# Attention values weighed per key head, high and low part side by side

## The chip, the cores and the metric

The kernel runs on one core of one Trainium2 chip. Its engines work side by side, each through its own list of instructions in order: TensorE (PE in the profile, its weight loads PEld), VectorE (DVE), ScalarE (ACT) and GpSimd (POOL); SyncE (SP) issues DMAs. They meet at semaphores. The metric is the device time of one execution in microseconds. Before the change it is 1051.31 us, the median of 3 runs (1051.22 to 1051.55).

## The reference

One decoder layer on 512 tokens of width 1024 in float32: a gated feed-forward half step, then pooling and attention side by side, merged by gates, then a second feed-forward half step. The change lies in attention, of which this is the core:

```python
q = rmsnorm(q, q_norm); k = rmsnorm(k, k_norm)          # 16 query heads, 2 key heads, width 64
# blocks of 128 queries; each sees its own 128 keys and the 128 before
scores = jnp.einsum('bnqhgd,bnkhd->bnhgqk', qb, kk) * (HEAD_DIM ** -0.5)
scores = jnp.where(mask, scores, finfo.min)
probs = softmax(concatenate([scores, sink], -1))[..., :-1]
out = jnp.einsum('bnhgqk,bnkhd->bnqhgd', probs, vv)     # the step that is changed
```

The result goes through w_attn_out, is gated, added to the pooling branch and multiplied by w_out.

## The kernel before

**Numbers in two parts.** The matmuls take operands in the format that the code calls F32R, not plain float32. Each matrix is split into a high part (the copy in that format, made by ScalarE) and a low part (what is left, made by VectorE or GpSimd), and a product takes three passes: high by high, high by low, low by high.

**Steps of attention.** The 512 tokens are four blocks of 128 queries (nb = 0 to 3). In each, four steps (j = 0 to 3) take four heads each: two query heads of either key head (kv). Block 0 has only its own 128 keys, the others 256. A step on TensorE (`step`, L909) is: the scores of step s (L877), half of a gate projection (24 products of 512 columns in all, L538 to L540), the turning of the probabilities of step s-1 (L891), the other half of the gate, and the weighing of the values by the probabilities of step s-1 (`weigh`, L894 to L907). The gate projections have nothing to do with attention's heads; they are work put between.

**The other engines in a step.** VectorE: maxima of the masked scores of step s (`maxima`, L1957 to L1973), low part of the turned probabilities of s-1 (L1998), denominators (L1978, L1980), scaling of the gate (L1985), and last the low part of the weighed values of s-1 (`attn_part`, L2005). In the step with j = 0 a copy of the block's factors (`rq_now`, L1950) comes ahead of the maxima. ScalarE: high part of the turned probabilities of s-1 (L1361), four exponentials of s (L1345), the high part of the next weights (L973), tanh of the gate (L1355), and last the high part of the weighed values of s-1 (L1367). GpSimd: the division of the probabilities (L1495), then the low part of the next weights (L1429), an instruction of about 2.4 us. Which engine does what, and in which order, is written out by hand in the code; the first and last blocks are written out, the middle ones run in a loop of the hardware.

**Weighing.** Before the change `weigh` multiplies both key heads at once. Of each half of the keys the stationary block holds the values of both key heads (128 columns), and the moving operand 512 columns of probabilities (2 key heads by 2 query heads by 128 queries). Only the rows of a key head that meet its own columns are used, so half of each product is thrown away. It waits for the low part of the turned probabilities (`pt_low`) and for the bank of the last step to be read out (`attn_low`).

**After attention.** TensorE begins the output projection (unit U_AO, L935 to L944) between the last steps: tiles 0 to 3 need the steps j = 0 and 1 of the last block, tiles 4 and 5 its step 2, tiles 6 and 7 its step 3. The wait ahead of the first tiles is L936.

Of the kernel before, what the change touches and what calls it, by code (L numbers as in the profile page):

```python
# [25 lines left out]
F32R = mybir.dt.float32r  # L26
ALU = mybir.AluOpType
ACT = mybir.ActivationFunctionType

P = 128  # L30
# [8 lines left out]
HD = 64  # L39
KV = 2  # L40
QT = 8
BLK = 128
NB = TOK // BLK
# [53 lines left out]
M_GATE_W = M_RINV + TOK * 4  # L97
# [24 lines left out]
def layer_kernel(nc, x_in, consts_in, params_in, poolw_in, weights_in, out):  # L122
    ctx = ExitStack()
    with ctx:
        def put(name, shape, at, dt=F32):

            return nc.alloc_sbuf_tensor_at(name, shape, dt, offset=at)

        def sem(name):
            return ctx.enter_context(nc.semaphore(name))  # L130
# [56 lines left out]
        m = M_GATE_W  # L187
        gate_w = blocks("gate", m, (m + 4096, m + 8192), m + 12288, m + 14336, (m + 16384, m + 18432),
                        m + 20480, m + 24576, m + 28672, m + 30720, m + 32768)
        m = M_RAW  # L190
# [10 lines left out]
        m = M_MIX  # L201
# [8 lines left out]
        m = m + 32768  # L210
# [4 lines left out]
        m = m + 6144  # L215
# [5 lines left out]
        m = m + 32768  # L221
# [10 lines left out]
        ks_l = put("k_block_low", [P, 2 * BLK], m + 21504, F32R)  # L232
        vs_h = put("v_block_high", [P, 2, P], m + 22528, F32R)
        vs_l = put("v_block_low", [P, 2, P], m + 23552, F32R)
        smax, msink, smx, nmax, rows, esink, den, rden = [
# [86 lines left out]
        pt_low = sem("pt_low_done")  # L322
        weighed = sem("weighed")
        attn_high = sem("attn_high_done")
        attn_low = sem("attn_low_done")
# [49 lines left out]
        def is_first(nb):  # L375
            return isinstance(nb, int) and nb == 0
# [5 lines left out]
        def halves(nb):  # L382

            return (1,) if is_first(nb) else (0, 1)

        def turned_count(nb, j):

            return j if is_first(nb) else 8 * nb - 4 + 2 * j

        def at(t, k, n=1):  # L390
# [141 lines left out]
        def _(pe):  # L532
# [361 lines left out]
            def weigh(nb, j):  # L894


                pe.wait_ge(pt_low, turned_count(nb, j) + len(halves(nb)))

                pe.wait_ge(attn_low, 8 * nb + 2 * j + 1)
                if j == 0:  # L900
                    pe.wait_ge(v_block_low, nb + 1)
                o = psum[:, 0, :]
                for k in halves(nb):
                    pe.matmul(o, vs_h[:, k, :], pt_h[:, k, :], start=(k == halves(nb)[0]), stop=False)  # L904
                    pe.matmul(o, vs_h[:, k, :], pt_l[:, k, :], start=False, stop=False)  # L905
                    mm = pe.matmul(o, vs_l[:, k, :], pt_h[:, k, :], start=False, stop=(k == 1))  # L906
                mm.then_inc(weighed, 1)  # L907
# [27 lines left out]
            pe.wait_ge(masked, 16 * NB + 1)  # L935
            pe.wait_ge(attn_low, 8 * NB - 3)  # L936
            project(U_AO, 0, 4, oh, ol, tiles=early)
# [3 lines left out]
            project(U_AO, 0, 4, oh, ol, tiles=range(TILES // 2, TILES - 2))  # L941
            pe.wait_ge(attn_low, 8 * NB + 1)
            project(U_AO, 0, 4, oh, ol, tiles=range(TILES - 2, TILES))
# [22 lines left out]
        def _(act):  # L966
# [298 lines left out]
            def stage_v(nb):  # L1265
                if not (isinstance(nb, int) and nb == 0):

                    act.wait_ge(weighed, 4 * nb)
                if is_first(nb):
                    act.activation(vs_h[:, 1, :], vtok[:, 1, :], ACT.Copy).then_inc(v_block_high, 1)  # L1270
                else:
                    act.activation(vs_h[:, :, :], vtok[:, bass.ds(nb, 2), :], ACT.Copy).then_inc(v_block_high, 1)

# [88 lines left out]

            def attn_part(nb, j):
                act.wait_ge(weighed, 4 * nb + j + 1)
                for kv in range(KV):
                    r = slice(kv * HD, (kv + 1) * HD)
                    act.activation(oh[r, 2 * j:2 * j + 2, bass.ds(nb * BLK, BLK)],  # L1367
                                   psum[r, 0, kv * 2 * BLK:(kv + 1) * 2 * BLK].rearrange("p (a t) -> p a t", a=2),
                                   ACT.Copy).then_inc(attn_high, 1)

# [54 lines left out]
        def _(pool):  # L1425
# [56 lines left out]
            def stage_v(nb):  # L1482
                pool.wait_ge(v_block_high, nb + 1)
                if is_first(nb):
                    pool.tensor_tensor(vs_l[:, 1, :], vtok[:, 1, :], vs_h[:, 1, :], ALU.subtract
                                       ).then_inc(v_block_low, 1)
                else:
                    pool.tensor_tensor(vs_l[:, :, :], vtok[:, bass.ds(nb, 2), :], vs_h[:, :, :],
                                       ALU.subtract).then_inc(v_block_low, 1)

# [34 lines left out]
        def _(dve):  # L1525
# [473 lines left out]

            def attn_part(nb, j):  # L2000
                for kv in range(KV):
                    dve.wait_ge(attn_high, 8 * nb + 2 * j + kv + 1)
                    r = slice(kv * HD, (kv + 1) * HD)
                    at_block = (r, slice(2 * j, 2 * j + 2), bass.ds(nb * BLK, BLK))
                    dve.tensor_tensor(ol[at_block],  # L2005
                                      psum[r, 0, kv * 2 * BLK:(kv + 1) * 2 * BLK].rearrange("p (a t) -> p a t", a=2),
                                      oh[at_block], ALU.subtract).then_inc(attn_low, 1)

# [165 lines left out]
```

## Time and profile before

| what | value |
| --- | --- |
| runs before | 1051.22, 1051.31, 1051.55 us |
| the profiled execution | 1052.04 us, its span 1050.1 us |
| TensorE busy, granted clock | 1039.5 us, 0.998 of full speed |
| VectorE, ScalarE, GpSimd busy | 653.3, 468.4, 432.3 us |
| attention's steps | about 474 to 617 us of the span |

The profiled execution is 0.7 us longer than the median, and 1.9 us of it lie outside the span. A matmul's busy time is longer than the distance at which matmuls follow each other, since they overlap: what one costs is read from the starts of two neighbours. On the other engines the length of a row is the time that the instruction held the engine, any stall inside it included; "[1.28 <-ACT ...]" is idle time before it and who ended it.

### The profile page before, as it was taken

The numbers are of one execution on the slowest core, as the hardware profiler recorded it, in microseconds if no ns is written. First come the engines' busy times: TensorE is split into PE (matmuls) and PEld (weight loads), VectorE is DVE, ScalarE is ACT, GpSimd is POOL, SyncE is SP. The second block draws the span as 40 slices with busy tenths as digits, with TensorE's granted clock in tenths as the row PEclk, the third lists the DMA queues.
The fourth block names the chain that finished last, engine by engine and source line by source line (L and its number), as shares of the span: only waits on it lengthen the run. The fifth ranks groups of instructions, "written<-read, shape, count | busy, mean of one in ns | idle before, by whom it ended". The sixth has DMA issues, their size and how long they took to land.

```text
span 1050.1 us, 15189 instructions
## 1 busy us (share of the span) xinstructions
PE 1039.5 (99%) x5934; PEld 905.4 (86%) x5934; DVE 653.3 (62%) x986; ACT 468.4 (45%) x810; POOL 432.3 (41%) x238
## 2 busy tenths in 40 slices
PE   9999999999999999999999999999999999999998
PEld 7878999998888888888778788888899999988887
DVE  6898777659340278426667656669987676594101
ACT  6442554455332243337677643344355554463210
POOL 1543423325434453345455544434424233354441
PEclk9999999999999999999999999999999999999999
DMA  6724757723222342222211123216367677233332
GB/s 208 218 83 125 184 152 184 193 76 120 92 91 98 131 140 81 81 81 82 62 59 60 61 81 100 95 60 176 93 165 184 172 185 187 91 103 98 100 100 100
DMA packets 42147, 124.80 MB, mean 119 GB/s; under 512 B 4320, under 2 KB 5344, under 8 KB 42080
## 3 DMA queue, kind: packets, MB, share of 16 engines
q1 hardware_dynamic: 37616, 107.89, 31.4%
q0 software_dynamic: 4320, 15.73, 8.7%
q8 instruction: 46, 0.75, 0.3%
q10 hardware_dynamic: 144, 0.26, 0.1%
q14 instruction: 21, 0.17, 0.1%
HBM read 121.76 MB, written 2.10 MB: 118 GB/s over the span
## 4 chain that ended last, share of the span: by engine, by line
PE 89%; DVE 7%; issue 1%; ACT 1%; DMA 1%; POOL 0%; SPq 0%; DVEq 0%; ACTq 0%
PE psum L538 19%; PE psum L539 18%; PE psum L540 18%; PE psum L641 10%; PE psum L642 10%; PE psum L643 10%; PE psum L877 1%; PE psum L891 1%; DVE u_blocks L1606 1%; DVE moving_sums_low L1631 1%; PE psum L785 1%; DMA up_s<-weights_dram 1%; PE psum L904 1%; PE psum L906 1%; PE psum L905 1%
## 5 line engine op out<-in xcount | busy, mean ns | idle before, releaser
L1429 POOL TENSOR_TENSOR w_low_in_place<-w_raw,w_high 128x1024 fp32r<-128x1024 f32 x68 | 170.5, 2509 | 210.1 <-ACT w_high L973 209.8
L973 ACT ACTIVATE w_high<-w_raw 128x1024 fp32r<-128x1024 f32 x118 | 124.5, 1055 | 220.5 <-DMA w_raw<-weights_dram 172.6
L1429 POOL TENSOR_TENSOR w_low<-w_raw,w_high 128x1024 fp32r<-128x1024 f32 x50 | 122.8, 2458 | 110.4 <-ACT w_high L973 110.4
L538 PE MATMUL psum<-hidden_high,w_high 128*128 128x512 f32 x352 | 137.0, 389 | 0.0
L539 PE MATMUL psum<-hidden_low,w_high 128*128 128x512 f32 x352 | 137.0, 389 | 0.0
L540 PE MATMUL psum<-hidden_high,w_low_in_place 128*128 128x512 f32 x352 | 136.9, 389 | 0.0
L1555 DVE SCALAR_TENSOR_TENSOR h<-psum,h 128x512 f32<-128x512 f32 x24 | 16.5, 689 | 151.0 <-PE psum L540 151.0
L538 PE MATMUL psum<-u_high,w_high 128*128 128x512 f32 x240 | 97.9, 408 | 0.0
L539 PE MATMUL psum<-u_low,w_high 128*128 128x512 f32 x240 | 93.8, 391 | 0.0
L540 PE MATMUL psum<-u_high,w_low 128*128 128x512 f32 x240 | 93.7, 390 | 0.0
L538 PE MATMUL psum<-ffn_u_high,w_high 128*128 128x512 f32 x222 | 88.2, 397 | 2.8 <-POOL w_low_in_place L1429 1.9
L540 PE MATMUL psum<-ffn_u_high,w_low_in_place 128*128 128x512 f32 x222 | 87.1, 392 | 0.0
L539 PE MATMUL psum<-ffn_u_low,w_high 128*128 128x512 f32 x222 | 86.9, 391 | 0.0
L540 PEld LDWEIGHTS psum<-hidden_high,w_low_in_place 128*128 128x128 f32 x352 | 66.1, 188 | 13.8
L538 PEld LDWEIGHTS psum<-hidden_high,w_high 128*128 128x128 f32 x352 | 66.1, 188 | 13.8
L539 PEld LDWEIGHTS psum<-hidden_low,w_high 128*128 128x128 f32 x352 | 66.1, 188 | 13.4
L1717 DVE TENSOR_TENSOR hidden_low<-hidden,hidden_high 128x512 fp32r<-128x512 f32 x44 | 63.6, 1501 | 12.8 <-ACT hidden_high L1042 12.8
L538 PEld LDWEIGHTS psum<-u_high,w_high 128*128 128x128 f32 x240 | 45.1, 188 | 10.8 <-issue 0.5
L1495 POOL TENSOR_TENSOR probs<-probs,inv_denominator 128x1024 f32<-128x1024 f32 (+1 forms) x16 | 26.9, 1682 | 66.4 <-DVE inv_denominator L1980 66.4
L540 PEld LDWEIGHTS psum<-u_high,w_low 128*128 128x128 f32 x240 | 45.1, 188 | 9.9
L538 PEld LDWEIGHTS psum<-ffn_u_high,w_high 128*128 128x128 f32 x222 | 42.1, 190 | 13.0 <-issue 4.4
L539 PEld LDWEIGHTS psum<-u_low,w_high 128*128 128x128 f32 x240 | 45.1, 188 | 8.7 <-issue 0.5
(261 smaller groups left out, 2828.9 us busy)
## 6 DMA issues: line engine op xcount, KB each, us to landing
w_raw<-weights_dram SPq DMA_DIRECT2D x118, 512.0 KB, 3.5
gate_a<-weights_dram SPq DMA_DIRECT2D x15, 512.0 KB, 6.0
gate_s<-weights_dram SPq DMA_DIRECT2D x15, 512.0 KB, 3.6
gate_s<-weights_dram POOLq DMA_DIRECT2D x15, 512.0 KB, 6.7
up_a<-weights_dram SPq DMA_DIRECT2D x15, 512.0 KB, 4.6
up_s<-weights_dram SPq DMA_DIRECT2D x15, 512.0 KB, 3.5
up_s<-weights_dram POOLq DMA_DIRECT2D x15, 512.0 KB, 8.1
gate_a<-weights_dram SPq DMA_DIRECT2D x15, 256.0 KB, 5.6
```

Source lines behind the costliest of these rows:

```text
L538: pe.matmul(o, wh, xh, start=start, stop=False)
L539: pe.matmul(o, wh, xl, start=False, stop=False)
L540: return pe.matmul(o, wl, xh, start=False, stop=stop)
L641: pe.matmul(o, wh[:, w], xh[:, c, :], start=fresh and c == 0, stop=False, skip_group_check=not fresh)
L642: pe.matmul(o, wh[:, w], xl[:, c, :], start=False, stop=False, skip_group_check=not fresh)
L643: mm = pe.matmul(o, wl[:, w], xh[:, c, :], start=False, stop=c == HALF - 1, skip_group_check=not fresh)
L785: mm = pe.matmul(psum[:, 2, col:col + KV], qsq[:, c % 2, b * BLK:(b + 1) * BLK], head_cols, start=True, stop=True, skip_group_check=True)
L973: act.activation(high[:, s, :], raw[:, s, :], ACT.Copy).then_inc(high_done, 1)
L1429: pool.tensor_tensor(wlow[:, s, :], raw[:, s, :], high[:, s, :], ALU.subtract).then_inc(low_done, 1)
L1495: pool.tensor_tensor(p, p, rden[:, j % 2, :].unsqueeze(2).to_broadcast([P, 4, width]), ALU.mult).then_inc(probs_ready, 1)
L1555: dve.scalar_tensor_tensor(out=tile(h, c), in0=psum[:, bank, :], scalar=scale, in1=tile(h, c), op0=ALU.mult, op1=ALU.add).then_inc(done, 1)
L1717: dve.tensor_tensor(hid_l[:, f, :], hid[:, f, :], hid_h[:, f, :], ALU.subtract).then_inc(F["hidden_low"], 1)
```

## The change

The stationary block now belongs to one key head: its 64 columns of high parts and its 64 columns of low parts stand side by side (`vs`, "v_block_parts"; for the second key head the low columns come first). The moving operand is that key head's 256 columns of probabilities, first their high part, then their low part. So a half of the keys takes four products of 256 columns in place of three of 512, and the product low by low, which was left out, is formed too. The result has the part from the high values on one half of the partitions and the part from the low values on the other; the two have to be added. For that ScalarE copies the parts from the low values to the partitions of their key head (`small_part`, two copies into "attn_now"), VectorE adds the parts from the high values (two sums), ScalarE makes the high part of all 128 partitions in one instruction, and VectorE the low part in one. Two semaphores are new, `attn_moved` and `attn_added`; `attn_low` now counts one for a step, where it counted two, and the waits that use it are rewritten. Ahead of the output projection the wait was for 8 NB - 3 = 29, that is the initial one and both instructions of 14 steps; it is now for 4 NB = 16, the initial one and 15 steps.

```diff
-        vs_h = put("v_block_high", [P, 2, P], m + 22528, F32R)
-        vs_l = put("v_block_low", [P, 2, P], m + 23552, F32R)
+        vs = put("v_block_parts", [P, 2, KV, P], m + 22528, F32R)
+        att = put("attn_now", [P, 2, BLK], M_GATE_W + 36864)
...
# TensorE, weigh
-                pe.wait_ge(attn_low, 8 * nb + 2 * j + 1)
+                pe.wait_ge(attn_low, 4 * nb + j + 1)
...
-                for k in halves(nb):
-                    pe.matmul(o, vs_h[:, k, :], pt_h[:, k, :], start=(k == halves(nb)[0]), stop=False)
-                    pe.matmul(o, vs_h[:, k, :], pt_l[:, k, :], start=False, stop=False)
-                    mm = pe.matmul(o, vs_l[:, k, :], pt_h[:, k, :], start=False, stop=(k == 1))
+                for kv in range(KV):
+                    cols = slice(kv * 2 * BLK, (kv + 1) * 2 * BLK)
+                    for k in halves(nb):
+                        first, last = k == halves(nb)[0], k == 1
+                        pe.matmul(psum[:, 0, cols], vs[:, k, kv, :], pt_h[:, k, cols], start=first, stop=False)
+                        mm = pe.matmul(psum[:, 0, cols], vs[:, k, kv, :], pt_l[:, k, cols], start=False, stop=last)
...
# TensorE, ahead of the output projection
-            pe.wait_ge(attn_low, 8 * NB - 3)
+            pe.wait_ge(attn_low, 4 * NB)
...
# ScalarE, stage_v: the same elements, written with a stride
-                    act.activation(vs_h[:, :, :], vtok[:, bass.ds(nb, 2), :], ACT.Copy).then_inc(v_block_high, 1)
+                    act.activation(high_parts(slice(0, 2)), by_kv(vtok[:, bass.ds(nb, 2), :]), ACT.Copy
+                                   ).then_inc(v_block_high, 1)
...
# ScalarE, at the end of a step
-            def attn_part(nb, j):
+            def small_part(nb, j):
+
                 act.wait_ge(weighed, 4 * nb + j + 1)
                 for kv in range(KV):
-                    r = slice(kv * HD, (kv + 1) * HD)
-                    act.activation(oh[r, 2 * j:2 * j + 2, bass.ds(nb * BLK, BLK)],
-                                   psum[r, 0, kv * 2 * BLK:(kv + 1) * 2 * BLK].rearrange("p (a t) -> p a t", a=2),
-                                   ACT.Copy).then_inc(attn_high, 1)
+                    r, other = slice(kv * HD, (kv + 1) * HD), slice((1 - kv) * HD, (2 - kv) * HD)
+                    cols = slice(kv * 2 * BLK, (kv + 1) * 2 * BLK)
+                    act.activation(att[r, :, :], psum[other, 0, cols].rearrange("p (a t) -> p a t", a=2), ACT.Copy
+                                   ).then_inc(attn_moved, 1)
+
+            def attn_part(nb, j):
+                small_part(nb, j)
+                act.wait_ge(attn_added, 8 * nb + 2 * j + 2)
+                act.activation(oh[:, 2 * j:2 * j + 2, bass.ds(nb * BLK, BLK)], att[:, :, :], ACT.Copy
+                               ).then_inc(attn_high, 1)
...
# VectorE, at the end of a step
             def attn_part(nb, j):
+
                 for kv in range(KV):
-                    dve.wait_ge(attn_high, 8 * nb + 2 * j + kv + 1)
-                    r = slice(kv * HD, (kv + 1) * HD)
-                    at_block = (r, slice(2 * j, 2 * j + 2), bass.ds(nb * BLK, BLK))
-                    dve.tensor_tensor(ol[at_block],
-                                      psum[r, 0, kv * 2 * BLK:(kv + 1) * 2 * BLK].rearrange("p (a t) -> p a t", a=2),
-                                      oh[at_block], ALU.subtract).then_inc(attn_low, 1)
+                    r, cols = slice(kv * HD, (kv + 1) * HD), slice(kv * 2 * BLK, (kv + 1) * 2 * BLK)
+                    dve.wait_ge(attn_moved, 8 * nb + 2 * j + 2)
+                    dve.tensor_tensor(att[r, :, :], psum[r, 0, cols].rearrange("p (a t) -> p a t", a=2),
+                                      att[r, :, :], ALU.add).then_inc(attn_added, 1)
+                dve.wait_ge(attn_high, 4 * nb + j + 1)
+                at_block = (slice(0, P), slice(2 * j, 2 * j + 2), bass.ds(nb * BLK, BLK))
+                dve.tensor_tensor(ol[at_block], att[:, :, :], oh[at_block], ALU.subtract).then_inc(attn_low, 1)
```

VectorE before, at the end of the second step (j = 1) of the last block: denominator, gate, the low parts of the weighed values, then the maxima of the next step.

```order
L1980 RECIPROCAL inv_denominator<-denominator 128x4 [waits den_done]
L1985 TENSOR_TENSOR squares<-psum,rinv 128x512 [waits unit_used]
L2005 TENSOR_TENSOR attn_low<-psum,attn_high 64x2x128 [waits attn_high_done] x2
L1957 MEMSET spare 128x1 [waits scored]
L1961 ISA probs,raw_max<-psum,consts 128x256
```

The same place in the changed kernel, whose line numbers are about 20 higher; "attn_now" is the new buffer.

```order
L2002 RECIPROCAL inv_denominator<-denominator 128x4 [waits den_done]
L2007 TENSOR_TENSOR squares<-psum,rinv 128x512 [waits unit_used]
L2027 TENSOR_TENSOR attn_now<-psum,attn_now 64x256 [waits attn_moved] x2
L2031 TENSOR_TENSOR attn_low<-attn_now,attn_high 128x2x128 [waits attn_high_done]
L1979 MEMSET spare 128x1 [waits scored]
L1983 ISA probs,raw_max<-psum,consts 128x256
```

Where two low parts stood, each waiting for ScalarE, two sums stand now, and behind them a low part of 128 partitions with a wait of its own. The maxima still come next in the row.

TensorE before, from the last product of the gate to the first of the output projection (the third step of the last block is weighed there).

```order
L540 MATMUL psum<-u_high,w_low 128x512
L904 MATMUL psum<-probsT_high,v_block_high 128x512 [waits attn_low_done,pt_low_done]
L905 MATMUL psum<-probsT_low,v_block_high 128x512
L906 MATMUL psum<-probsT_high,v_block_low 128x512
L904 MATMUL psum<-probsT_high,v_block_high 128x512
L905 MATMUL psum<-probsT_low,v_block_high 128x512
L906 MATMUL psum<-probsT_high,v_block_low 128x512
L538 MATMUL psum<-attn_high,w_high 128x512 [waits low_done,attn_low_done,masked]
```

The same place in the changed kernel.

```order
L553 MATMUL psum<-u_high,w_low 128x512
L919 MATMUL psum<-probsT_high,v_block_parts 128x256 [waits attn_low_done,pt_low_done]
L920 MATMUL psum<-probsT_low,v_block_parts 128x256
L919 MATMUL psum<-probsT_high,v_block_parts 128x256
L920 MATMUL psum<-probsT_low,v_block_parts 128x256
L919 MATMUL psum<-probsT_high,v_block_parts 128x256
L920 MATMUL psum<-probsT_low,v_block_parts 128x256
L919 MATMUL psum<-probsT_high,v_block_parts 128x256
L920 MATMUL psum<-probsT_low,v_block_parts 128x256
L551 MATMUL psum<-attn_high,w_high 128x512 [waits low_done,attn_low_done,masked]
```

Six products of 512 columns became eight of 256. The first product of the output projection waits for the same semaphores as before, but `attn_low` now has to count the very step that was weighed just ahead of it.

## Rows read from the trace of the kernel before

**Rows 1.** The page, busy time, share of the span and instructions of each engine.

```profile
PE 1039.5 (99%) x5934; PEld 905.4 (86%) x5934; DVE 653.3 (62%) x986; ACT 468.4 (45%) x810; POOL 432.3 (41%) x238
```

**Rows 2.** Chain that ended last, around a block's end: start, length, engine, tile, line.

```profile
574.02 0.36 ACT attn_high L1367
...
575.44 1.53 DVE rq_now L1950
...
580.46 0.49 PE psum L904
```

**Rows 3.** Timeline of ScalarE, third block: start, length, instruction, [idle before, releaser].

```profile
556.26 0.77 ACT L1367 ACTIVATE attn_high<-psum 64x256 f32 x2
...
559.83 1.09 ACT L1361 ACTIVATE probsT_high<-psum 128x512 fp32r<-128x512 f32 x2 [2.80 <-PE psum L891]
...
560.81 0.60 ACT L1345 ACTIVATE probs<-probs,neg_max,rq_now 128x256 f32<-128x256 f32 x1
...
565.17 0.77 ACT L1367 ACTIVATE attn_high<-psum 64x256 f32 x2
```

**Rows 4.** Timeline of VectorE, the same step.

```profile
556.78 0.88 DVE L2005 TENSOR_TENSOR attn_low<-psum,attn_high 64x256 f32 x2 [1.28 <-ACT attn_high L1367]
...
559.77 0.15 DVE L1973 TENSOR_TENSOR sink_minus_max<-params,score_max 128x4 f32<-128x4 f32 x1
```

**Rows 5.** Timeline of GpSimd, four of its weight instructions.

```profile
481.64 2.39 POOL L1429 TENSOR_TENSOR w_low<-w_raw,w_high 128x1024 fp32r<-128x1024 f32 x1
...
488.15 2.40 POOL L1429 TENSOR_TENSOR w_low<-w_raw,w_high 128x1024 fp32r<-128x1024 f32 x1
...
556.82 2.41 POOL L1429 TENSOR_TENSOR w_low<-w_raw,w_high 128x1024 fp32r<-128x1024 f32 x1
...
574.54 2.40 POOL L1429 TENSOR_TENSOR w_low<-w_raw,w_high 128x1024 fp32r<-128x1024 f32 x1
```

**Rows 6.** Timeline of VectorE, one small sum while GpSimd is busy.

```profile
482.02 2.02 DVE L1967 TENSOR_TENSOR score_max<-raw_max,rq_now 128x4 f32<-128x4 f32 x1
```

**Rows 7.** Line 1950, VectorE: duration in ns, shortest/median/longest.

```profile
L1950 DVE COPY rq_now<-rq x4: 174/1208/1528, 467.5 to 575.4; 128x16 f32<-128x16 f32 x2, 128x16 f32 x2
```

**Rows 8.** Groups by form, 483 to 619 us: busy us, mean ns, idle before.

```profile
L2005 DVE TENSOR_TENSOR attn_low<-psum,attn_high 64x256 f32 x16 | 6.8, 422 | 11.1 <-ACT attn_high L1367 10.9
...
L1272 ACT ACTIVATE v_block_high<-v_tokens 128x256 fp32r<-128x256 f32 x1 | 0.4, 418 | 0.0
```

**Rows 9.** Timeline of TensorE, products of 512 and of 256 columns.

```profile
553.51 0.39 PE L904 MATMUL psum<-probsT_high,v_block_high 128*128 128x512 f32 x1
...
553.74 0.39 PE L905 MATMUL psum<-probsT_low,v_block_high 128*128 128x512 f32 x1
...
909.06 0.28 PE L641 MATMUL psum<-u_blocks_high,gate_a_high 128*128 128x256 f32 x1
...
909.18 0.28 PE L642 MATMUL psum<-u_blocks_low,gate_a_high 128*128 128x256 f32 x1
```

**Rows 10.** ScalarE, the first turn, the fourth and the last but one.

```profile
488.38 0.77 ACT L1367 ACTIVATE attn_high<-psum 64x256 fp32r<-64x256 f32 x2
...
511.88 0.76 ACT L1367 ACTIVATE attn_high<-psum 64x256 fp32r<-64x256 f32 x2
...
609.85 0.77 ACT L1367 ACTIVATE attn_high<-psum 64x256 fp32r<-64x256 f32 x2
```

**Rows 11.** Timeline of VectorE, the first block.

```profile
488.77 0.88 DVE L2005 TENSOR_TENSOR attn_low<-psum,attn_high 64x256 fp32r<-64x256 f32 x2 [1.12 <-ACT attn_high L1367]
...
491.90 0.69 DVE L1998 TENSOR_TENSOR probsT_low<-psum,probsT_high 128x512 fp32r<-128x512 f32 x1 [0.52 <-ACT probsT_high L1361]
```

**Rows 12.** Timeline of TensorE, the end of attention.

```profile
608.53 0.39 PE L538 MATMUL psum<-attn_high,w_high 128*128 128x512 f32 x1
...
614.86 0.39 PE L904 MATMUL psum<-probsT_high,v_block_high 128*128 128x512 f32 x1
...
617.76 0.50 PE L538 MATMUL psum<-attn_high,w_high 128*128 128x512 f32 x1
```

More of the change, by code:

```diff
@@ L323, in layer_kernel @@
         weighed = sem("weighed")
+        attn_moved = sem("attn_moved")
+        attn_added = sem("attn_added")
         attn_high = sem("attn_high_done")
@@ L388, in turned_count, with high_parts, low_parts, by_kv @@
             return j if is_first(nb) else 8 * nb - 4 + 2 * j
+        def high_parts(k):
+            return vs[:, k, :, :].rearrange("p k v n -> p k (v n)").rearrange("p k (a n) -> p k a n", n=HD)[:, :, 0:4:3, :]
+        def low_parts(k):
+            return vs[:, k, :, :].rearrange("p k v n -> p k (v n)").rearrange("p k (a n) -> p k a n", n=HD)[:, :, 1:3, :]
+        def by_kv(t):
+            return t.rearrange("p k (a n) -> p k a n", n=HD)
         def at(t, k, n=1):
@@ L897, in weigh @@
                 pe.wait_ge(pt_low, turned_count(nb, j) + len(halves(nb)))
-                pe.wait_ge(attn_low, 8 * nb + 2 * j + 1)
+                pe.wait_ge(attn_low, 4 * nb + j + 1)
                 if j == 0:
                     pe.wait_ge(v_block_low, nb + 1)
-                o = psum[:, 0, :]
-                for k in halves(nb):
-                    pe.matmul(o, vs_h[:, k, :], pt_h[:, k, :], start=(k == halves(nb)[0]), stop=False)
-                    pe.matmul(o, vs_h[:, k, :], pt_l[:, k, :], start=False, stop=False)
-                    mm = pe.matmul(o, vs_l[:, k, :], pt_h[:, k, :], start=False, stop=(k == 1))
+                for kv in range(KV):
[4 more added lines that the diff above has]
+                        mm = pe.matmul(psum[:, 0, cols], vs[:, k, kv, :], pt_l[:, k, cols], start=False, stop=last)
                 mm.then_inc(weighed, 1)
@@ L941, in _ @@
             project(U_AO, 0, 4, oh, ol, tiles=range(TILES // 2, TILES - 2))
-            pe.wait_ge(attn_low, 8 * NB + 1)
+            pe.wait_ge(attn_low, 4 * NB + 1)
             project(U_AO, 0, 4, oh, ol, tiles=range(TILES - 2, TILES))
@@ L1269, in stage_v @@
                 if is_first(nb):
-                    act.activation(vs_h[:, 1, :], vtok[:, 1, :], ACT.Copy).then_inc(v_block_high, 1)
-                else:
-                    act.activation(vs_h[:, :, :], vtok[:, bass.ds(nb, 2), :], ACT.Copy).then_inc(v_block_high, 1)
+                    act.activation(high_parts(slice(1, 2)), by_kv(vtok[:, 1:2, :]), ACT.Copy
+                                   ).then_inc(v_block_high, 1)
+                else:
+                    act.activation(high_parts(slice(0, 2)), by_kv(vtok[:, bass.ds(nb, 2), :]), ACT.Copy
+                                   ).then_inc(v_block_high, 1)
             def pooled_part(g):
@@ L1484, in stage_v @@
                 if is_first(nb):
-                    pool.tensor_tensor(vs_l[:, 1, :], vtok[:, 1, :], vs_h[:, 1, :], ALU.subtract
-                                       ).then_inc(v_block_low, 1)
-                else:
-                    pool.tensor_tensor(vs_l[:, :, :], vtok[:, bass.ds(nb, 2), :], vs_h[:, :, :],
-                                       ALU.subtract).then_inc(v_block_low, 1)
+                    k, v = slice(1, 2), vtok[:, 1:2, :]
+                else:
+                    k, v = slice(0, 2), vtok[:, bass.ds(nb, 2), :]
+                pool.tensor_tensor(low_parts(k), by_kv(v), high_parts(k), ALU.subtract).then_inc(v_block_low, 1)
             def normalize(nb, j):
```

## The prediction

> **What bounds the kernel now.** I began with the page's busy shares: TensorE is at work for 99% of the span [rows 1], so work taken from it seems to be time won. But these shares cover stages with different limits, so I went to the stage of the change next, to the chain of waits. At the end of a block it leaves TensorE: it runs over ScalarE's high part of the weighed values, VectorE's copy of the block's factors and the low part of the turned probabilities, and only then comes back to TensorE's weighing [rows 2]. So here TensorE is waited for and waits. The timelines of the two engines show the ring behind it, in which TensorE has no part:
>
> ScalarE's `attn_part` of step s-1, then VectorE's, then the maxima of step s+1 (next in VectorE's order), then ScalarE's exponentials of s+1, its weights and gate, and `attn_part` of step s.
>
> I measure it from one `attn_part` on ScalarE to the next, in a plain step of the third block. ScalarE starts at 556.26 [rows 3]; VectorE's two low parts run from 556.78 to 557.66 and its maxima are done at 559.92 [rows 4]. The exponentials could start 3.66 after the first instant, plus about 0.05 for the signal. They start at 560.81, since ScalarE first takes the turned probabilities, for which it waited until 559.83 [rows 3]. From the exponentials to the next `attn_part`, at 565.17, are 4.36 us. So the ring alone needs 3.71 + 4.36 = 8.07 us, and the step takes 8.91: 0.84 us of slack for anything put into the ring. That is the figure against which the change has to be held.
>
> **What TensorE gains.** Neighbouring products of 512 columns start 0.23 us apart, of 256 columns 0.12 us [rows 9]. A weighing costs 6 x 0.2275 = 1.37 us now and 8 x 0.12 = 0.96 afterwards: 0.41 less in each of 12 steps, and half of it in the four of the first block (3 products become 4): 12 x 0.405 + 4 x 0.20 = 5.7 us. This is all that the change can give.
>
> **What the ring gets.** Where before two high parts and two low parts overlapped, five hand-overs now stand one behind the other. From the start t of ScalarE's first copy:
> - two copies out of the bank, as the two high parts now: 0.77 [rows 3]; as many partitions and columns, and the shift of partitions, which no row shows, I price at nothing.
> - two sums on VectorE, one operand in the bank, as the two low parts now: 0.88 [rows 4]. They wait for both copies. For the signal between engines, half of ScalarE's pair lasts 0.385, and VectorE began 0.52 after its start in the loop (556.78 after 556.26, rows 3, 4) and 0.39 in a block that is written out (488.77 after 488.38, rows 10, 11): 0.14 and next to nothing.
> - one high part of 128 x 256: 0.42, as line 1272 [rows 8].
> - one low part of 128 x 256: 0.42, as line 2005 [rows 8], whose columns are the same.
>
> With three signals of 0.02 to 0.14 the low part is ready to start at t + 2.13 to t + 2.49. It was finished at t + 1.40 before.
>
> **Where the low part is held.** Its operands both lie in SBUF now; before, one lay in the bank. GpSimd's low part of the weights starts 0.56 after t and lasts 2.41, to t + 2.97 [rows 5]. The old low parts ran inside it unhurt at 0.42 each [rows 4]. But a sum of four columns with both operands in SBUF, begun at 482.02, ended at 484.04, when GpSimd's instruction begun at 481.64 ended (484.03) [rows 5, 6]; and the copy of the factors, 0.17 us when free [rows 7], took 1.53 and ended at 576.97, with GpSimd's of 574.54 to 576.94 [rows 2, 5]. So I let the new low part wait to t + 2.97 and end at t + 3.39.
>
> The Trainium skill (SBUF — State Buffer, "SBUF: two separate sides") says the same as a rule: VectorE with two SBUF inputs and GpSimd lock a shared pair of ports for a whole instruction, and the later one waits. The stalls just shown agree. By it the sum is the one below; without it, the first rival's.
>
> **The sum.** New ring: 3.39, then maxima 2.26 (from the end of the low parts, 557.66 to 559.92), signal 0.05, and 4.36: 10.06 us, 1.15 over the step of today and 1.99 over the ring of today. TensorE would need 8.5, so its 0.41 buys nothing and it waits at each weighing.
> - Eleven turns with 256 keys lie between ScalarE's `attn_part` at 511.88 and that at 609.85 [rows 10]: 97.97 us. Then 11 x 10.06 = 110.7, plus 0.2 in each of two block ends for the copy of the factors, which GpSimd no longer holds up there because the low part has already waited for it: 111.1. That is +13.1.
> - Three turns begin in the first block, from 488.38 to 511.88. There GpSimd ends at 490.55, t + 2.17 [rows 5, 10]; the low part ends at t + 2.6, where it ended at t + 1.27 [rows 11]: 1.33 later, less the 0.52 that VectorE still waited behind its maxima [rows 11]. Three times 0.8: +2.4.
> - The end. Today the output projection starts at 608.53 [rows 12], 1.32 before ScalarE's `attn_part` of step 2 of the last block (609.85, rows 10), since its wait asks only for the steps before. Now it asks for that step too: it can start at t + 3.39 + 0.05, which is 4.8 us later relative to the ring. TensorE has nothing else in its order ahead of it.
> - From there to tiles 6 and 7 are 9.23 us today, of which 6.33 lie ahead of the last weighing (614.86) [rows 12]. After: 6.33, the weighing 1.12 to the end of its last product, then 0.77 + 0.88 + 0.42 + 0.42 with signals 0.1 (GpSimd has no work there in its order until the next weights are used), and 0.05: 10.1. That is +0.9, with TensorE's gain in the last weighing already in it.
>
> Together 13.1 + 2.4 + 4.8 + 0.9 = +21.2 us. On the profiled execution's 1052.04 that is 1073.2; the median lies 0.7 lower, so I say 1072.5. Behind attention TensorE is busy again almost without a gap, so nothing gives this back.
>
> Hidden, and priced at nothing: the strided split of the values has the same elements on ScalarE and GpSimd, and it moves about 1.5 us later in its step behind the new wait, while the weighing that needs it comes most of a step later. No DMA is issued or moved; SyncE and GpSimd keep their order. ScalarE, blocked inside `attn_part` until VectorE has added, has idle time there today, 2.80 us ahead of L1361 [rows 3].
>
> **Bounds.** Low: the low part isn't held and signals cost 0.02: it ends at t + 2.55, a ring of 9.2, 11 turns +3.5 (with the copy of the factors held as today), the first block +2.4, the end 3.9 + 0.9: +10.7, 1062. High: at three block starts GpSimd's low part of the values (256 columns, by a quarter of the 2.41 for 1024 [rows 5] some 0.7) goes first, and once that of the keys: +2.8; and TensorE's clock falls in the new waits. The granted clock is 0.998 over this span, which is its level of 2.4 GHz, so no row prices that; for the 12 products ahead of the turning I take twice their 2.7 us: +2.7. That gives +26.7, 1078.
>
> **The rivals.**
> First, the low part isn't held by GpSimd: the ring is bound all the same, at 9.2 to 9.6, and the whole comes to +11 to +15, 1064. For it: no instruction of just this form runs beside GpSimd in this stage. Against it: both stalls above.
> Second, more stalls, as in the upper bound: 1077. What speaks for it is that GpSimd's next piece is often ready; against it, that the low part has waited longer.
> Third, the other side: the ring has room after all, and TensorE's 5.7 us come out, 1045.6. It needs the five hand-overs to cost under 0.84 us more than the overlapped pairs; by the rows they cost at least 1.15 (2.55 against 1.40), and the wait ahead of the output projection must be met early, while it asks for a step weighed just before. A little room would give a zero.
> That products of 256 columns don't save what they should changes little: TensorE waits in this stage, and only the 0.4 us of the last weighing would go.
>
> **How the numbers follow.** Forecast 0.62 (its own range 1068 to 1076), first rival 0.20, second 0.12, faster 0.04, no change 0.02. The range 1062 to 1078 takes in the first two rivals. A difference of 0.2%, some 2 us, is about what a measurement of this kernel can tell from none: faster 0.04, same 0.02, slower 0.94.
>
> **What would show it.** Right: ten-microsecond steps between 512 and 630; TensorE waiting over 1 us for L1998's successor ahead of each weighing and about 5 us for `attn_low` ahead of the output projection; the new low part lasting about 0.9 and ending with GpSimd's instruction; exponentials starting right behind the maxima. Wrong: low parts of 0.42 beside GpSimd (first rival), steps of 8.5 us (third), or a time under 1053.

## The result, and the profile after

The changed kernel takes 1072.54 us (median of 4 runs, 1072.09 to 1074.46), against 1051.43 us for the kernel before (4 runs): a ratio of 1.0206, 95% interval 1.0191 to 1.0220. The profiled execution took 1072.94 us, 20.9 more than that of before, and its span is 1071.1 us. The forecast was 1072.5.

The page's first line after, to be held against [rows 1]. TensorE is busy 2.5 us less in a span that is 21 us longer.

```profile
PE 1037.0 (97%) x5962; PEld 904.1 (84%) x5962; DVE 662.0 (62%) x1002; ACT 476.3 (44%) x826; POOL 432.9 (40%) x238
```

Where the time went is read first from one step to the next. Here is the timeline of ScalarE after, the first turn, the fourth and the last but one, which answer to [rows 10] (start, length, instruction; L1385 is the first half of the new `attn_part`).

```profile
488.60 0.79 ACT L1385 ACTIVATE attn_now<-psum 64x256 f32<-64x256 f32 x2
...
514.84 0.78 ACT L1385 ACTIVATE attn_now<-psum 64x256 f32<-64x256 f32 x2
...
622.72 0.78 ACT L1385 ACTIVATE attn_now<-psum 64x256 f32<-64x256 f32 x2
```

The first three turns take 26.24 us where they took 23.50, the next eleven 107.88 where they took 97.97: 2.7 and 9.9 us more. One plain turn of the loop, on ScalarE:

```profile
564.20 0.78 ACT L1385 ACTIVATE attn_now<-psum 64x256 f32<-64x256 f32 x2
566.02 0.42 ACT L1391 ACTIVATE attn_high<-attn_now 128x256 f32 x1 [1.04 <-DVE attn_now L2027]
...
569.51 0.60 ACT L1361 ACTIVATE probs<-probs,neg_max,rq_now 128x256 f32<-128x256 f32 x1 [1.39 <-DVE sink_minus_max L1995]
...
574.00 0.78 ACT L1385 ACTIVATE attn_now<-psum 64x256 f32<-64x256 f32 x2
```

The same turn on VectorE, where [rows 4] had one pair of low parts.

```profile
565.01 0.88 DVE L2027 TENSOR_TENSOR attn_now<-psum,attn_now 64x256 f32<-64x256 f32 x2 [1.69 <-ACT attn_now L1385]
566.59 0.71 DVE L2031 TENSOR_TENSOR attn_low<-attn_now,attn_high 128x256 f32 x1 [0.71 <-ACT attn_high L1391]
...
569.32 0.16 DVE L1995 TENSOR_TENSOR sink_minus_max<-params,score_max 128x4 f32<-128x4 f32 x1
```

And GpSimd's low part of the weights in that turn.

```profile
564.64 2.39 POOL L1452 TENSOR_TENSOR w_low<-w_raw,w_high 128x1024 fp32r<-128x1024 f32 x1
```

With t = 564.20 the sums start at t + 0.81, the high part at t + 1.82, the low part at t + 2.39; it ends at t + 3.10, and GpSimd at t + 2.83. Then come the maxima, and right behind them the exponentials, which now wait for VectorE. The turn takes 9.80 us.

TensorE waits accordingly. These rows are the waits between 480 and 660 us (engine and line, what they waited for: us in all, times, longest; PEld and PE show the same stalls).

```profile
ACT probs L1361 <- DVE sink_minus_max L1995: 19.6, 15, 2.1
...
PEld psum L919 <- DVE probsT_low L2020: 15.6, 11, 1.5
PE psum L919 <- DVE probsT_low L2020: 14.7, 13, 2.3
...
PE psum L551 <- issue: 5.2, 1, 5.2
...
PE psum L551 <- DVE attn_low L2031: 1.3, 1, 1.3
```

The last two stand at the end of attention, where [rows 12] had no wait: ahead of the output projection and ahead of its tiles 6 and 7. TensorE's timeline there:

```profile
625.95 0.76 PE L551 MATMUL psum<-attn_high,w_high 128*128 128x512 f32 x1 [5.17 <-issue]
...
626.94 0.63 PE L553 MATMUL psum<-attn_high,w_low 128*128 128x512 f32 x1
627.37 0.63 PE L551 MATMUL psum<-attn_high,w_high 128*128 128x512 f32 x1
...
629.42 0.39 PE L553 MATMUL psum<-attn_high,w_low 128*128 128x512 f32 x1
...
633.98 0.28 PE L919 MATMUL psum<-probsT_high,v_block_parts 128*128 128x256 f32 x1
...
637.79 0.50 PE L551 MATMUL psum<-attn_high,w_high 128*128 128x512 f32 x1 [1.30 <-DVE attn_low L2031]
```

The first wait has no releaser in the trace ("issue"); e1 below shows that it is the one for `attn_low`. Behind it the products start 0.43 apart, not 0.23. The granted clock tells why (stretch, its length, busy times of the engines; the number behind the last "(x..)" is the clock):

```profile
625.90:627.00 1.10, 1.05 (x3) 0.89 (x4) 0.00 (x0) 0.00 (x0) 0.00 (x0) 0.50 0.42 45
...
629.00:630.00 1.00, 1.00 (x5) 0.79 (x4) 0.00 (x0) 0.00 (x0) 0.00 (x0) 0.85 0.00 0
630.00:631.00 1.00, 1.00 (x9) 0.86 (x8) 0.00 (x0) 0.00 (x0) 0.00 (x0) 1.00 0.00 0
```

After 5.17 us without work TensorE got its lower level, 1.2 GHz, until about 629.3. The first eight products took 3.47 us (625.95 to 629.42); the eight behind the shorter wait, at the full clock, took 1.97.

The 21.0 us of span add up so: the first turn starts 0.2 later, the fourteen turns take 12.65 more, the projection starts 3.23 behind ScalarE's `attn_part` where it started 1.32 ahead of it (4.55), from there to tiles 6 and 7 are 11.84 us where there were 9.23 (2.61), and 1.0 lies behind, where nothing was edited.

### The profile page after: what moved, and what is told of

Its sections match the earlier page's. It is cut to its first block, busy times and chain, and to the rows that moved or that the text cites. A ratio compares the mean times of both kernels' runs of the same rounds, so it can differ in the third digit from the quotient of the medians.

```text
span 1071.1 us, 15259 instructions
## 1 busy us (share of the span) xinstructions
PE 1037.0 (97%) x5962; PEld 904.1 (84%) x5962; DVE 662.0 (62%) x1002; ACT 476.3 (44%) x826; POOL 432.9 (40%) x238
## 4 chain that ended last, share of the span: by engine, by line
PE 76%; DVE 12%; ACT 5%; issue 4%; DMA 1%; POOL 0%; DVEq 0%; SPq 0%; ACTq 0%
PE psum L551 16%; PE psum L552 16%; PE psum L553 16%; PE psum L654 9%; PE psum L656 9%; PE psum L655 9%; ACT probs L1361 2%; DVE probs L1983 1%; DVE attn_now L2027 1%; ACT attn_now L1385 1%; DVE u_blocks L1628 1%; DVE squares L2007 1%; DMA gate_a<-weights_dram 1%; DVE moving_sums_low L1653 1%; PE psum L798 1%
```

## The experiments

In each, "turns" is the time from ScalarE's first `attn_part` to its last but one, and "wait" is TensorE's wait ahead of the output projection, both from the profiled execution. Medians are to be compared by their ratios, since e1 to e4, e5 to e8, and e9 and e10 have their own runs of before (1050.17, 1051.59 and 1051.04 us).

| kernel | turns, us | wait, us | median, us | ratio to before, 95% interval |
| --- | --- | --- | --- | --- |
| before | 121.47 | none | 1051.43 | 1 |
| the change | 134.12 | 5.17 | 1072.54 | 1.0206 (1.0191 to 1.0220) |
| e1, projection earlier | 134.12 | none | 1064.11 | 1.0124 (1.0105 to 1.0143) |
| e2, products twice | 134.32 | 4.22 | 1073.48 | 1.0216 (1.0188 to 1.0243) |
| e3, short weights | 130.70 | 4.62 | 1068.91 | 1.0175 (1.0150 to 1.0201) |
| e4, low part behind the maxima | 120.91 | 4.92 | 1059.16 | 1.0075 (1.0051 to 1.0099) |
| e5, e4 and e1 together | 120.85 | none | 1051.20 | 1.0004 (0.9992 to 1.0015) |
| e6, before with a short delay | 121.48 | none | 1052.82 | 1.0019 (1.0008 to 1.0031) |
| e7, before with a long delay | 127.10 | none | 1058.12 | 1.0060 (1.0045 to 1.0074) |
| e8, e5 and two moves | 118.57 | none | 1047.04 | 0.9963 (0.9951 to 0.9975) |
| e9, before with one of them | 120.34 | none | 1049.54 | 0.9985 (0.9976 to 0.9994) |
| e10, e8 again | 118.62 | none | 1047.01 | 0.9962 (0.9949 to 0.9976) |

**e1: the output projection asks for one step less.**

```diff
-            pe.wait_ge(attn_low, 4 * NB)
+            pe.wait_ge(attn_low, 4 * NB - 1)
```

> The changed kernel (1072.5 us), with the wait ahead of the output projection one count lower, so that it asks for the steps that its first tiles use. Theory of the ring and the late wait: of the 21 us, 15 come from longer steps and 6 from this one wait, during which TensorE stands still for 5.2 us and then runs 3 us at half its granted clock (0.50 between 626 and 629 us). So about 6 us come back: 1066.5 us (1065.5 to 1067.5), and the granted clock stays at 1.00 there. Rival, the ring alone: the step that is waited for is late anyway, and TensorE waits as long a little further on: 1071 to 1073 us.

TensorE in that kernel goes from the weighing into the projection without a pause, and the clock stays at 1.00; its last wait is as long as before.

```profile
619.43 0.28 PE L920 MATMUL psum<-probsT_low,v_block_parts 128*128 128x256 f32 x1
619.55 0.40 PE L551 MATMUL psum<-attn_high,w_high 128*128 128x512 f32 x1
```

```profile
630.11 0.50 PE L551 MATMUL psum<-attn_high,w_high 128*128 128x512 f32 x1 [1.30 <-DVE attn_low L2031]
```

Tiles 6 and 7 start 7.68 us earlier, 1.06 of it because the first turn does (487.54). So the rewritten wait cost 6.6 us, its half-clock products with it, and the turns, the same to a hundredth, most of the rest. By the ratios it was more (0.82%, 8.6 us, with intervals of 2 us on either side), which puts e1 below the 1065.5 that I had given as its lower bound.

**e2: every product of the weighing twice**, so that the weighed values come out twice as large and TensorE has eight more products in a step.

```diff
                         pe.matmul(psum[:, 0, cols], vs[:, k, kv, :], pt_h[:, k, cols], start=first, stop=False)
+                        pe.matmul(psum[:, 0, cols], vs[:, k, kv, :], pt_l[:, k, cols], start=False, stop=False)
+                        pe.matmul(psum[:, 0, cols], vs[:, k, kv, :], pt_h[:, k, cols], start=False, stop=False)
```

> The changed kernel with each weighing's products made twice (16 of 256 columns in place of 8, half of that in the first block; the weighed values come out too large). Theory of the ring: TensorE waits 1.07 us or more ahead of each weighing, so the 0.96 us are hidden in every step but the last weighing, behind which it is waited for: 1073.0 to 1074.0 us. Rival, TensorE still sets the steps: 12 x 0.96 + 4 x 0.48 = 13.4 us more, 1086 us.

The turns grow by 0.2 us in all, and the waits ahead of the weighing shrink instead (in its trace between 480 and 660 us; 15.6 in the changed kernel):

```profile
PEld psum L919 <- DVE probsT_low L2022: 6.3, 11, 0.9
```

So TensorE's work in a step is not what lasts; the rival, a step bound by TensorE, falls.

**e3: GpSimd makes the low part of only half the columns of the gate weights** in these steps (the other half is left as it was in the buffer).

```diff
-                low_part(U_GATE + SLOTS + SLOTS * nb + j, j)
+                low_part(U_GATE + SLOTS + SLOTS * nb + j, j, cols=slice(0, UNIT // 2))
```

> The changed kernel, in which GpSimd makes the low part of only half of the next weights in the steps of attention (512 of 1024 columns; the other half of these low parts is left out). Its instruction then ends before VectorE's new low part starts. Theory: the low part falls from 0.68 (loop) and 1.00 (last block) to 0.43 us, the steps get shorter by 0.25 and by 0.57 us: about 7 x 0.25 + 5 x 0.57 = 4.5 us less, 1068 us (1067 to 1069.5). Rival, GpSimd's port makes most of the loss: 1060 us or less. Rival, the port has no part in it: 1072.5 us.

The low part of the weighed values, over all 16 steps (shortest, median and longest in ns), first in the changed kernel, then in this one:

```profile
L2031 DVE TENSOR_TENSOR attn_low<-attn_now,attn_high x16: 424/678/1015, 490.8 to 637.3; 128x256 fp32r<-128x256 f32 x8, 128x256 f32 x8
```

```profile
L2031 DVE TENSOR_TENSOR attn_low<-attn_now,attn_high x16: 424/426/427, 489.4 to 632.4; 128x256 fp32r<-128x256 f32 x8, 128x256 f32 x8
```

Where it started before the end of GpSimd's 2.4 us instruction it was held; beside one of 1.29, which has ended by then, it is not. The hold is real, and worth 3.4 of the 12.65 us of the turns (the ratios, 1.0175 and 1.0206, have intervals that overlap, so this rests on the turns). The other 9.2 are the five hand-overs themselves: a plain turn still takes 9.52 us.

**e4: VectorE makes the low part behind the next maxima** instead of ahead of them.

```diff
+            def attn_low_part(nb, j):
...
                 maxima(nb, j)
+                if not (is_first(nb) and j < 2):
+                    attn_low_part(*((nb, j - 2) if j >= 2 else (nb - 1, j + 2)))
                 turned_part(*before)
```

> The changed kernel with one instruction of each step moved: VectorE's low part of the weighed values stands behind the maxima of the next step, where it stood ahead of them; the two sums stay in their place. Theory of the ring: the copy and the low part fall out of it, about 1.4 us, and it needs 8.4 to 8.6 us, about what TensorE needs: the steps come to 8.5 to 8.6 us, two block ends to 9.7, so attention's steps are some 3 us shorter than in the kernel before; the late wait ahead of the output projection stays, with 7 us: 1055.5 us (1053 to 1058). Rival, the extra instructions themselves cost (0.8 us more work on ScalarE and VectorE in each step, wherever they stand): 1069 to 1073 us.

The turns go back to 120.91 us: out of the ring, the low part costs nothing there. That is the theory's direction, but I had expected 3 us less, and the time is 3.7 above what I gave, out of its range of 1053 to 1058: the block ends still take 9.46 us, held by the copy of the factors, and the step with the block's staging 9.07. The wait ahead of the projection stays:

```profile
612.30 0.77 PE L551 MATMUL psum<-attn_high,w_high 128*128 128x512 f32 x1 [4.92 <-issue]
...
624.72 0.50 PE L551 MATMUL psum<-attn_high,w_high 128*128 128x512 f32 x1 [1.30 <-DVE attn_low L2034]
```

**e5: e4's and e1's edits together.**

> The change with both repairs: VectorE's low part behind the next maxima, and TensorE's wait ahead of the output projection asking for one step less. Both theories start from the two measured apart: the low part behind the maxima gave 1059.16 where the change alone gave 1072.54, the shorter wait took 7.7 us off the start of the later tiles. Theory (the ring and the end are two separate costs): they add up, the 4.92 us of waiting ahead of the projection go, with them about 1.6 us of products at half clock, so 1059.2 - 6.6 = 1052.6, ratio 1.000 to 1.004; the steps stay as they were with the low part moved (120.9 us from 488 to 609). Rival (the wait only moves, since the turning behind the projection waits for the same ring): 1057 to 1059.

The two costs add up. Counted from the first turn, tiles 6 and 7 start 7.26 us earlier than in e4 (615.98 after 486.67, against 624.72 after 488.15), and the kernel takes as long as before (1.0004). With both repairs nothing of the loss is left, but of the up to 5.7 us that TensorE saves nothing is seen either.

**e6 and e7: the kernel before, with VectorE held up between its two low parts**, by one copy of 256 columns (about 0.4 us; e6) or two of 512 (e7). The copies go into buffers that nobody reads.

```diff
                 for kv in range(KV):
                     dve.wait_ge(attn_high, 8 * nb + 2 * j + kv + 1)
+                    if kv == 1:
+                        dve.tensor_copy(extra[:, :], psum[:, 0, :])
+                        dve.tensor_copy(other[:, :], psum[:, 0, :])
```

> The kernel before, with one more copy of 128x256 from the bank (about 0.4 us) between VectorE's two low parts of the weighed values: it lengthens the ring by 0.4 and nothing else; TensorE's work is that of before. Theory (the ring of before has 0.84 us of slack in a step of the loop): steps of 8.9 remain in the loop, at most 0.4 us in the three block ends and 0.4 at the last step: 0 to +2 us, 1050.2 to 1052.2. Rival (no slack, each step takes the delay whole): 15 x 0.4 = +6, 1056.

> The kernel before, with two more copies of 128x512 from the bank (about 0.65 us each, 1.3 together) at the same place. Theory (slack of 0.84 in a step, of which 1.3 uses all and adds the rest): 0.5 us in each of nine steps, 0.8 in each of three block ends, 1.3 behind the last step: +8, between +5 and +11, 1055 to 1061. Rival one (TensorE alone sets the steps): only the last step shows it, +1.4, 1051.6. Rival two (no slack): 15 x 1.3 = +20, 1070.

In e6 the turns take 121.48 us, against 121.47: a delay of 0.42 in each of them vanishes whole. The ratio, 1.0019, is some 2 us, at the upper end of the expectation; the profiled execution (1051.51 us) shows none of them. They go along with the granted clock: the three runs of e6 at 1.000 took 1050.31 to 1051.51 us, the seven at 0.998 or 0.999 took 1052.73 to 1056.16 (before: eight of 23 below 1.000); why there were more of them is not shown. In e7, VectorE's timeline in a plain turn:

```profile
568.92 0.42 DVE L2010 TENSOR_TENSOR attn_low<-psum,attn_high 64x256 f32 x1 [1.32 <-ACT attn_high L1369]
569.26 0.67 DVE L2006 COPY extra<-psum 128x512 f32<-128x512 f32 x1
569.86 0.67 DVE L2007 COPY other<-psum 128x512 f32<-128x512 f32 x1
570.55 0.43 DVE L2010 TENSOR_TENSOR attn_low<-psum,attn_high 64x256 f32 x1
```

The pair ends 2.06 us after its start where it took 0.88, so the delay is 1.18. ScalarE's plain turns take 9.23 (559.18 to 568.41 to 577.64) where they took 8.91 and 8.85: 0.32 and 0.38 more. So 0.80 to 0.86 us of the delay went into slack; the prediction had read 0.84 from the timelines of before. The six turns between 512 and 578 us that are no block ends now take 9.23 to 9.28, which is the prediction's ring of 8.07 and the delay of 1.18 together; two of them that had taken only 8.58 and 8.67 grew by 0.66 and 0.61, so there the slack was about 0.5 to 0.6. Both rivals, TensorE alone and no slack, fall. The two block ends of the loop took none of it, where I had expected 0.8 each: there the copy of the factors had been held for 1.53 us by GpSimd [rows 2], and the delay now stands in that time. At the first block end, where that copy had been held for only 0.90, 0.53 was left of it.

```profile
580.24 0.35 DVE L1952 COPY rq_now<-rq 128x16 f32 x1
```

**e8: e5, and two moves more.** Tiles 4 and 5 of the projection's second unit go ahead of TensorE's last wait, and the copy of the next block's factors to the end of the last step, where VectorE waits anyway.

```diff
             project(U_AO, 0, 4, oh, ol, tiles=range(TILES // 2, TILES - 2))
+            project(U_AO + 1, 1, 5, oh, ol, tiles=range(TILES // 2, TILES - 2))
             pe.wait_ge(attn_low, 4 * NB + 1)
             project(U_AO, 0, 4, oh, ol, tiles=range(TILES - 2, TILES))
-            project(U_AO + 1, 1, 5, oh, ol, tiles=late)
+            project(U_AO + 1, 1, 5, oh, ol, tiles=range(TILES - 2, TILES))
...
-                if j == 0:
-                    block_factors(nb)
                 maxima(nb, j)
...
                 gate(nb, j)
+                if j == SLOTS - 1 and not (isinstance(nb, int) and nb == NB - 1):
+                    block_factors(nb + 1)
                 attn_part(*before)
```

> As the kernel with both repairs, and two moves more: tiles 4 and 5 of the projection's second unit stand ahead of TensorE's wait for the last step, and VectorE copies the next block's factors at the end of the block's last step instead of at the start of the next. Theory: the tiles cover the 1.3 us of waiting for the last low part, and each of the two block ends in the loop gets about 1.1 us shorter, if VectorE gets the port between GpSimd's instructions: 1 to 3.5 us under the kernel with both repairs, 1047 to 1051.5. Rival (the copy is held by GpSimd's weights just the same, and delays the sums behind it): only the 1.3 us, or nothing.

This version is a little faster than both kernels: 0.9963 of before (0.9951 to 0.9975), and 4.2 us under e5, where I had given 1 to 3.5. VectorE and GpSimd at the end of a block:

```profile
569.99 1.47 DVE L1973 COPY rq_now<-rq 128x16 f32 x1
571.80 0.88 DVE L2028 TENSOR_TENSOR attn_now<-psum,attn_now 64x256 f32<-64x256 f32 x2 [0.34 <-ACT attn_now L1386]
```

```profile
569.54 1.90 POOL L1518 TENSOR_TENSOR probs<-probs,inv_denominator 128x1024 f32<-128x1024 f32 x1 [3.11 <-DVE inv_denominator L2003]
571.39 2.39 POOL L1453 TENSOR_TENSOR w_low<-w_raw,w_high 128x1024 fp32r<-128x1024 f32 x1
```

The copy is held as before, now by the division of the probabilities, but its end at 571.46 is still ahead of what VectorE has to wait for. The two block ends of the loop fall from 9.46 to 8.48, the first from 8.67 to 8.36 (2.28 us of turns), and TensorE's last wait is gone (1.30): 3.6 of the 4.2 us.

**e9 and e10: is it the change?** e9 is the kernel before with the move of `block_factors` alone (the second part of the diff above); e10 is e8 again, beside it.

> The kernel before with one edit: VectorE copies the next block's factors at the end of the block's last step, ahead of its low parts, instead of at the start of the next. It asks how much of the 3.7 us by which the kernel with three moves lies under before needs the change at all. Theory (the change saves TensorE time, which the repairs let through): here only the block ends get shorter, the two in the loop from 9.47 to at least 8.9 us, since the ring itself stays, and the first by at most as much: 1 to 1.8 us in all, 1049.8 to 1050.6 on 1051.6, a ratio of 0.998 to 0.999. Rival (the gain was the copy alone): 0.9963 again.

> The kernel with three moves once more, on the chip and beside the runs of the control. Theory: 0.996 to 0.997 of before, about 2 us under the control. Rival (the difference to before was drift of that hour): within 0.2% of before, and not under the control.

The move alone gives 1.5 us (0.6 to 2.5; its two block ends of the loop take 8.82, a little under the 8.9 that I had expected at least); e8 gives 4.0, the same ratio as the first time. So some 2.5 us belong to the change with its repairs (1.7 by the turns, 118.62 against 120.34), under half of the 5.7 that TensorE could save at most. The move of the tiles, which e9 leaves out, can hardly make up the difference: in the kernel before, tiles 6 and 7 start 0.40 us behind the product ahead of them (617.76, rows 12), where neighbours are 0.23 apart, so it could win 0.17 there.

```profile
617.36 0.39 PE L540 MATMUL psum<-attn_high,w_low 128*128 128x512 f32 x1
```

Where the ring leaves the saving free it shows: three turns of the written-out last block take 25.33 us in e10 (579.48 to 604.81) and 26.51 in e9 (581.01 to 607.52).

## Why the prediction was right, and where its sum was off

- **The ring.** Its order was as told: copies, sums, high part, low part, maxima, exponentials. The low part was ready at t + 2.39 (forecast 2.13 to 2.49). That the ring of the kernel before needs 8.07 us and leaves 0.84 of slack in a plain turn, on which all else rests, e7 has measured.
- **The hold by GpSimd.** Right in kind, too large in size. Its instruction began at t + 0.44, not t + 0.56, and so ended at t + 2.83, not t + 2.97; and the held low part ended 0.27 behind it, not its full 0.42. Thus 0.71 us in place of 0.9, a turn of 9.75 to 9.80 in place of 10.06, and 9.9 us for the eleven turns where 13.1 stood. The first block's 2.4 were 2.7. This part of the sum was 2.85 us too high. The rule of the Trainium skill (SBUF — State Buffer, "SBUF: two separate sides") agrees with the hold: when e3 shortened GpSimd's instruction, the low part took 0.42. It doesn't give the size: if the low part had waited for the whole instruction and only then begun, 0.42 would have stood behind GpSimd's end, not 0.27; why it was less stays open. And of the two stalls with which the prediction matched it, only the sum of four columns has two operands in SBUF; the copy of the factors has one, and was held all the same.
- **The wait ahead of the projection.** Forecast 4.8, measured 4.55; e1 took it out and gave it back.
- **The end.** From the start of the last weighing to tiles 6 and 7 are 3.81 us (633.98 to 637.79), forecast 3.77. But the twelve products and the turning ahead of it took 8.03 in place of 6.33. The prediction had the half clock as part of its upper bound only, at 2.7; it came, and cost about 1.5. So +0.9 became +2.6.
- **Behind attention.** Priced at nothing, measured +1.0. From tiles 6 and 7 to the end of the span are 433.3 us here and 432.3 before, and kernels that are alike in this stretch differ by as much (432.3 in e4, 433.5 in e5), so I don't put it down to the change.
- **The total.** The ring was 2.85 too high, the wait 0.25 too high; the end 1.7 and the rest 1.2 too low. That the sum met the time to a tenth is luck: errors of about 3 us either way cancel. Either side alone would have left it inside the range.
- **The rivals.** The first, no hold, can be read in e3: a turn of 9.52, inside its 9.2 to 9.6, but 1.0175 in all, some 18 us where it gave 11 to 15: from the projection's start to tiles 6 and 7, where products at half the clock stand, e3 takes 12.21 us, 2.98 over before, where the prediction had 0.9, and 1.6 lie outside attention. The second, more stalls, needed GpSimd's low part of the values to go ahead of VectorE's; it came behind it (517.01 and 517.70 in the last section), and no low part lasted longer than 1.02 us. Of its two parts only the clock came, with 1.5 of its 2.7 us. The third, room in the ring, needed the hand-overs to cost under 0.84 us a turn; even without the hold, e3's turns are 9.2 us longer than those of before in all.

## What to carry to other kernels

Before work is taken from a busy engine, follow the ring of hand-overs through the other engines and read its slack from two timelines: here 0.84 us in a plain turn decided, not TensorE's 99%. A result that only a far consumer needs (the low part) belongs behind what the ring waits for next, and a semaphore that counts differently has to be checked for which step each wait now asks. When the repaired version comes out at zero, look for the next held instruction in the ring: here the copy of the factors kept 2.3 us.

## What the runs showed of the hardware

A single wait of 5.17 us left TensorE at half its clock for about 3.4 us of work, and those of 4.22, 4.62 and 4.92 us in e2, e3 and e4 left it at 0.50 too. In e1, whose longest pause at that place is 1.30 us, the granted clock is 1.00; and in the changed kernel a wait of 2.32 us ahead of a weighing left it at 1.00 (521.60 to 523.00).

```profile
521.62 0.38 PE L919 MATMUL psum<-probsT_high,v_block_parts 128*128 128x256 f32 x1 [2.32 <-DVE probsT_low L2020]
```

Between two instructions of GpSimd that follow each other VectorE got its turn: in the changed kernel its low part of 517.01 ended 0.28 behind the first of them, and the second took 0.93 where the same instruction takes 0.74 elsewhere (554.49 in e3).

```profile
517.01 1.01 DVE L2031 TENSOR_TENSOR attn_low<-attn_now,attn_high 128x256 fp32r<-128x256 f32 x1 [0.48 <-ACT attn_high L1391]
```

```profile
515.35 2.39 POOL L1452 TENSOR_TENSOR w_low<-w_raw,w_high 128x1024 fp32r<-128x1024 f32 x1
517.70 0.93 POOL L1511 TENSOR_TENSOR v_block_parts<-v_tokens,v_block_parts 128x256 fp32r<-128x256 f32 x1
```
